# Which half of the tokens is combined first in the tail of a decoder layer, and how the gates of the dense experts are built

## The reference

```python
def peer_ffn(xf, w_query, keys1, keys2, expert_u, expert_v):
    def block(xt):                                    # 128 tokens
        qry = (xt @ w_query).reshape(PEER_BLOCK, PEER_HEADS, 2, PEER_KEY_DIM)
        s1 = jnp.einsum('thd,kd->thk', qry[:, :, 0], keys1)
        s2 = jnp.einsum('thd,kd->thk', qry[:, :, 1], keys2)
        v1, i1 = lax.top_k(s1, PEER_TOPK)
        v2, i2 = lax.top_k(s2, PEER_TOPK)
        cand_s = (v1[..., :, None] + v2[..., None, :]).reshape(PEER_BLOCK, PEER_HEADS, PEER_TOPK * PEER_TOPK)
        cand_i = (i1[..., :, None] * PEER_KEYS + i2[..., None, :]).reshape(...)
        top_s, pos = lax.top_k(cand_s, PEER_TOPK)
        idx = jnp.take_along_axis(cand_i, pos, axis=-1)
        gate = jax.nn.softmax(top_s.astype(jnp.float32), axis=-1).astype(xt.dtype)
        act = jax.nn.gelu(jnp.einsum('td,thkd->thk', xt, expert_u[idx]))
        return jnp.einsum('thk,thkd->td', gate * act, expert_v[idx])
```

## Time and profile before

| what | value |
|---|---|
| median of the timed runs | 4261.98 us |
| the profiled execution's own time | 4251.53 us |
| its span (what all rows below refer to) | 4249.7 us |
| PE busy | 3756.1 us, 88% |
| DVE busy | 2619.1 us, 62% |
| POOL busy | 1856.3 us, 44% |
| ACT busy | 811.9 us, 19% |
| moved by DMA | 1063.93 MB, 250 GB/s on the mean |
| software (indirect) DMA | 537.08 MB |

### The profile page before, as it was taken

One profiled execution on the slowest core, in us unless ns is written; L12 is line 12 of the kernel. 1 busy time (PEld: TensorE's weight loads), 2 busy tenths in 40 slices (PEclk: granted clock), 3 DMA queues, 4 the chain that ended last, 5 costly groups with the idle time before them and its releaser, 6 DMA issues. The chain is left out here.

```text
span 4249.7 us, 42972 instructions
## 1 busy us (share of the span) xinstructions
PE 3756.1 (88%) x15498; PEld 2778.5 (65%) x15498; DVE 2619.1 (62%) x5356; ACT 811.9 (19%) x1637; POOL 1856.3 (44%) x1714
## 2 busy tenths in 40 slices
PE   8889998978999999993697899989789999999935
PEld 7546787867766666641585467877676666666424
DVE  5765216645577677788657652166456776677876
ACT  2243302224000000000222532022240000000002
POOL 6102004764455455567370020047645554555663
PEclk9889999989999999996798999999899999999967
DMA  3201144558999999999722012345579999999996
GB/s 103 109 30 40 66 139 119 125 142 268 376 406 409 409 407 409 407 397 378 266 82 109 31 39 76 139 119 124 159 253 397 405 410 409 401 409 409 399 381 253
DMA packets 333955, 1063.93 MB, mean 250 GB/s; under 512 B 79152, under 2 KB 96176, under 8 KB 312496
## 3 DMA queue, kind: packets, MB, share of 16 engines
q0 software_dynamic: 184320, 537.08, 34.5%
q1 hardware_dynamic: 132368, 505.22, 31.5%
q10 hardware_dynamic: 17056, 18.88, 1.3%
HBM read 1025.27 MB, written 35.78 MB: 250 GB/s over the span
## 5 line engine op out<-in xcount | busy, mean ns | idle before, releaser
L2091 POOL DMA_INDIRECT u_rows<-in_peer_u,idx_all x512 | 662.7, 1294 | 681.1 <-DVE act_u L1990 564.3
L1657 PE MATMUL bank<-v_tile,shared 128*128 128x512 f32 x2048 | 904.6, 597 | 25.3 <-DVE shared L2032 22.5
L2002 DVE SCALAR_TENSOR_TENSOR x<-v_rows,act_w,x 128x1024 f32<-128x1024 f32 x512 | 657.9, 1285 | 345.0 <-DMA v_rows<-in_peer_v,idx_all 325.9
L2091 POOL DMA_INDIRECT v_rows<-in_peer_v,idx_all x512 | 545.7, 1066 | 402.2 <-DVE x L2002 309.8
L1657 PEld LDWEIGHTS bank<-v_tile,shared 128*128 128x128 f32 x2048 | 392.0, 192 | 476.5 <-issue 444.3
L1990 DVE CUSTOM_DVE_ANT_0 u_rows<-u_rows,h 128x1024 f32<-128x1024 f32 x512 | 609.2, 1223 | 146.1 <-DMA u_rows<-in_peer_u,idx_all 144.7
L2101 POOL DMA_INDIRECT first_cells<-first_gate,cell_all x256 | 412.1, 1610 | 578.0 <-DVEq L1982 465.3
L1645 PE MATMUL bank<-hT,bT 128*128 128x256 f32 x2048 | 454.4, 381 | 0.0
L1645 PEld LDWEIGHTS bank<-hT,bT 128*128 128x128 f32 x2048 | 391.1, 191 | 73.6 <-issue 23.9
L1549 PE MATMUL bank<-hT,ring 128*128 128x256 f32 x1536 | 341.3, 384 | 14.2 <-PEq L150 14.2
L1549 PEld LDWEIGHTS bank<-hT,ring 128*128 128x128 f32 x1536 | 294.3, 193 | 55.9 <-issue 15.8
(11 more groups left out here) (377 smaller groups left out, 4998.9 us busy)
## 6 DMA issues: line engine op xcount, KB each, us to landing
v_tile<-in_peer_v SPq DMA_DIRECT2D x256, 512.0 KB, 7.5
ring<-in_w_in_panels SPq DMA_DIRECT2D x76, 1024.0 KB, 4.9
bT<-in_peer_ut SPq DMA_DIRECT2D x128, 512.0 KB, 7.5
ring<-in_peer_w_query SPq DMA_DIRECT2D x32, 1024.0 KB, 5.0
aT<-in_peer_ut SPq DMA_DIRECT2D x64, 512.0 KB, 6.9
sT<-in_peer_ut SPq DMA_DIRECT2D x64, 512.0 KB, 6.8
ring<-in_ple_w_gate SPq DMA_DIRECT2D x24, 1024.0 KB, 8.4
first_cells<-zeros SPq DMA_DIRECT2D x16, 1024.0 KB, 11.4
```

What stands on the lines that cost most here:

```text
L1657: ins = mm(acc[t][part][:, :], act_pair[p % AHEAD][:, at:at + P], v_tile[:, e % DENSE, part * 512:part * 512 + 512], start=(e == 0), stop= ...
L2002: stt(out=m.x[:, 2 + t, :], in0=vr[:, n % RINGS, :], scalar=act_w[:, p % 4, i:i + 1], in1=m.x[:, 2 + t, :], op0=ALU.mult, op1=ALU.add).the ...
L2091: nc.gpsimd.indirect_dma_start(out=rows[:, n % RINGS, :], out_offset=None, in_=table, in_offset=bass.IndirectOffsetOnAxis(ap=idx_all[:, t, ...
```

## The change

1. Half 1, the gathered one, is combined first. Its first two heads are chosen early in the combination of half 0, so that chunks 0 to 10 stand between the steps of that combination and chunk 11 behind its norm. The fetches of POOL stand in the same places of the list.
2. The eight heads of half 0 are then chosen in a row, with six `pre` between them.
3. Both tiles of half 0 get their gates from one-hot products: 64 quads instead of 32, with two chunks between them. The scatter, the cell numbers and the zeros are gone, and the reads of the scattered table too. DVE now compares and scales in one instruction per token; every third quad's other side is made by ACT (Square, then Relu of one minus it).
4. The third head of half 1 is chosen among the six late `pre`; chunks 15 to 65 follow with the 64 pairs as before, so 41 chunks instead of 52 stand beside the pairs.
5. ACT's gelu of a chunk is moved one chunk later in the list. DVE applies the gates of a pair in one instruction instead of two, and SP loads the first two groups of gates after `pre` 8.

The core of the diff:

```diff
-QUADS = P // 4
-HOT_CHUNKS = 4
+QUADS = 2 * P // 4
+HOT_CHUNKS = 15
+ACT_QUAD = 2
 LAG = 2
+GATES_AFTER = 8
+GATHER, DENSE_HALF = 1, 0
+FIRST_HEADS = 2
...
+    g, d = steps[GATHER], steps[DENSE_HALF]
+    order = g + d[0:1] + [("norm", GATHER)] + d[1:2] + [("query", GATHER, 0), ("query", GATHER, 1)] + d[2:3] + [("score", GATHER, 0)]
+    order += choose(GATHER, 0) + d[3:5] + [("score", GATHER, 1)] + choose(GATHER, 1) + d[5:6] + chunk(0) + d[6:7] + chunk(1)
+    begun = 2
+    for n in range(7, 20):
+        order += d[n:n + 1]
+        if n % 4 != 2 and n != 11:
+            order += chunk(begun)
+            begun += 1
+    order += [("norm", DENSE_HALF), ("query", DENSE_HALF, 0), ("query", DENSE_HALF, 1), ("score", DENSE_HALF, 0)] + chunk(begun)
+    begun += 1
     pairs = 0
+    for head in range(PEER_HEADS):
+        order += [("query", DENSE_HALF, head + 2)] if head + 2 < PEER_HEADS else []
+        order += [("score", DENSE_HALF, head + 1)] if head + 1 < PEER_HEADS else []
+        order += choose(DENSE_HALF, head)
+        if pairs < EARLY:
+            order.append(("pre", pairs))
+            pairs += 1
+    order.append(("slots",))
     for q in range(QUADS):
         order.append(("hot", q))
+        if q % 20 == 19 and begun < HOT_CHUNKS - 1:
+            order += chunk(begun)
+            begun += 1
+    order += [("hot", QUADS), ("query", GATHER, FIRST_HEADS), ("score", GATHER, FIRST_HEADS)]
     for p in range(pairs, AHEAD):
         order.append(("pre", p))
+        if p == GATES_AFTER:
+            order.append(("first_gates",))
+        if p == pairs + 1:
+            order += choose(GATHER, FIRST_HEADS)
...
@@ hot, on ACT
-                    act.wait_ge(s.left_ready, q + 1)
+                k = q + 2
+                if k < QUADS and by_act(k):
+                    if k >= 4:
+                        act.wait_ge(s.hot_filled, k - 3)
+                    tile, at = k // (P // 4), 4 * k % P
                     for i in range(4):
-                        at = 4 * q + i
-                        f(left[q % 4][:, i, :], left[q % 4][:, i, :], ACT.Copy, scale=turned_sel[:, 2, at:at + 1]).then_inc(s.left_scaled, 1)
+                        f(right[k % 4][:, i, :], m.c("iota"), ACT.Square, scale=-1.0, bias=turned_sel[:, tile, 0, at + i:at + i + 1]).then_inc(s.right_squared, 1)
+                    act.wait_ge(s.right_squared, 4 * right_made(k)[1])
+                    f(right[k % 4], right[k % 4], ACT.Relu, scale=-1.0, bias=1.0).then_inc(s.right_acted, 1)
@@ hot, on DVE
-                tt(left[q % 4], over(turned_sel[:, 1, at:at + 4].unsqueeze(2), (P, 4, P)),
-                   over(m.c("iota").unsqueeze(1), (P, 4, P)), ALU.is_equal).then_inc(s.left_ready, 1)
-                tt(right[q % 4], over(turned_sel[:, 0, at:at + 4].unsqueeze(2), (P, 4, P)),
-                   over(m.c("iota").unsqueeze(1), (P, 4, P)), ALU.is_equal).then_inc(s.right_ready, 1)
+                for i in range(4):
+                    ts(left[q % 4][:, i, :], m.c("iota"), turned_sel[:, tile, 1, at + i:at + i + 1], first_gate[:, tile, at + i:at + i + 1],
+                       ALU.is_equal, ALU.mult).then_inc(s.left_ready, 1)
+                if not by_act(q):
+                    tt(right[q % 4], over(turned_sel[:, tile, 0, at:at + 4].unsqueeze(2), (P, 4, P)),
+                       over(m.c("iota").unsqueeze(1), (P, 4, P)), ALU.is_equal).then_inc(s.right_ready, 1)
@@ on POOL
-            late = TOPK * (PEER_HEADS - 1)
-            for n in range(late):
-                scatter(n)
```

More of the change, by code:

```diff
@@ L1368, in tail_order @@
[L1368 to L1385, removed]
@@ L1387, in tail_order @@
-    pairs = 0
+    place = {what: k for k, what in enumerate(CHOSEN)}
+    choose = lambda half, head: [("choose", place[half, head], part) for part in range(4)]
+    beside = {}
+    for head in range(FIRST_HEADS + 2, PEER_HEADS):
+        at = HEAD_CHUNKS * (head - 1) - (4 if head == PEER_HEADS - 1 else 0)
+        beside.setdefault(at - 5, []).append(("query", GATHER, head))
+        beside.setdefault(at - 2, []).append(("score", GATHER, head))
+        for part in range(4):
+            beside.setdefault(at + part, []).append(("choose", place[GATHER, head], part))
@@ new lines, in chunk @@
+    def chunk(c):
+        return beside.pop(c, []) + [("chunk", c)]
+    g, d = steps[GATHER], steps[DENSE_HALF]
[7 more added lines that the diff above has]
+            begun += 1
@@ L1396, in tail_order @@
     for p in range(pairs, AHEAD):
         order.append(("pre", p))
+        if p == GATES_AFTER:
+            order.append(("first_gates",))
+        if p == pairs + 1:
+            order += choose(GATHER, FIRST_HEADS)
+    while begun < HOT_CHUNKS:
+        order += chunk(begun)
+        begun += 1
+    for n, what in enumerate([("query", GATHER, FIRST_HEADS + 1), ("score", GATHER, FIRST_HEADS + 1)] + choose(GATHER, FIRST_HEADS + 1)):
+        beside.setdefault(begun + n, []).append(what)
     after = {DENSE_END: [("add",), ("embed", 0)], DENSE_END + 1: [("scale", 0), ("turn", 0)], DENSE_END + 2: [("turned", 0)]}
@@ L1558, in mix @@
             def mix(half, pair):
-                if half == 0 and pair == 0:
+                if rank(half) == 0 and pair == 0:
                     pe.wait_ge(s.wg_in, 16)
@@ L1582, in norm @@
             def norm(half):
-                for t in range(2 * half, 2 * half + 2):
-                    pe.wait_ge(s.h_ready, t + 1)
+                for t in range(2):
+                    pe.wait_ge(s.h_ready, 2 * rank(half) + t + 1)
                     for part, banks in ((0, to_act), (1, to_vec)):
@@ L1593, in query @@
             def query(half, head):
-                if half == 0 and head == 0:
+                if rank(half) == 0 and head == 0:
                     pe.wait_ge(s.keys_in, 16 * 2)
@@ L1751, in _ @@
             loads = iter(range(len(sources)))
-            parts = {"gate": panel, "mix": panel, "out": panel, "query": panel, "embedded": panel, "pre": pre, "values": values, "add": add}
+            parts = {"gate": panel, "mix": panel, "out": panel, "query": panel, "embedded": panel, "pre": pre,
+                     "first_gates": first_gates, "values": values, "add": add}
             for what, *n in order:
@@ L2117, in _ @@
                     fetch(n, s.v_free, vr, tables[1], m.v_landed)
-                if c < LATE_CHUNKS:
-                    for n in range(TOPK // LATE_CHUNKS):
-                        scatter(late + c * TOPK // LATE_CHUNKS + n)
+            parts = {"norm": norm, "chunk": chunk}
+            for what, *n in order:
+                if what in parts:
+                    parts[what](*n)
     clear(nc, s)
```

199 lines of the change are left out of this document (77 added, 122 removed).

## The result

The changed kernel takes 4428.02 us, the median of four runs (4427.25 to 4432.55), against 4261.1 for the kernel before on the same chip: 1.0395 times as long, interval 1.0377 to 1.0413. The forecast was 4290, with a range up to 4350. So the direction came true, and the change was +167 us where the sum had +28, six times as much.

The account below looks back on a forecast made before the run. DMA was taken to hold PE back by some 52 us in the pairs. Per layer +101 - 42 - 45 = +14, +28 for two on 4251.5, gave 4280, as a median 4290; own range 4262 to 4320, with rivals 4210 to 4350.

Parts of the forecast that it names:

- the sum: All terms of a layer's tail together: +101 - 42 - 45 = +14 us, for two layers +28.
- The first combination and the first choice: Start of the tail: combination unchanged, first choice about 15 us later, near 2802; the mix costs PE about 11 us.
- The second combination: Combination with early chunks: DVE's order binds, 146 us, plus 18 for DMA, up to 3010; then eight choices, quads from 3142.
- rival 4: Second combination: gathers beside it crawl, so it doesn't overlap as said; chance 0.07 together with rival 3.
- The quads: 64 quads at 1.3 us, with chunks, cold starts and staging waits 106 us, bounds 76 and 155.
- rival 3: Quads: the clock stays low throughout, 149 us instead of 106, +57 a layer, 4376; chance 0.07 together with rival 4.
- From the quads to the first `values`: Behind the quads: a query, a score and seven `pre` pairs on PE take 56 us, up to 3304.
- the front: Start of the tail to the first `values`: 101 us later per layer, at 3304 against 3202.7.
- the term of -42: Stage of pairs: PE becomes the bound at 795 us, with 10 allowed for late tiles, against 847 taken.
- The term of -45: Behind PE's last product: the dense sums are added on DVE 2 us later instead of 47.
- Rival 2: Stage of pairs: DMA stays the bound, PE loses 30 us, sums 15 later; 4380, half of it 4335; chance 0.11.
- Rival 1: Quads: they run at PE's own pace, 76 us instead of 106; 4230, or 4194 clear of the DMA limit; chance 0.32.

Follow-up runs that it names:

- c1: a3 with 6 instead of 15 early chunks ahead of the pairs: 4381.39 us, ratio 1.0296.
- c3: a3 with three of four parts of the last four dense choices left out (computes other gates, only prices the choices): 4309.89 us, ratio 1.0128.
- e1: a3 with the chunk ahead of the first dense choice and the two in the quads moved behind the quads: 4352.53 us, ratio 1.0234.
- a1_goal: The changed kernel with chunks 15 to 56 and the pairs spread by PE's work (a pair with `pre` counts 2, without 1): 4366.89 us, ratio 1.0266.
- a2: The changed kernel with the gelu back in its own chunk's place from chunk 15 on: 4421.34 us, ratio 1.0387.
- a3: The changed kernel with the edits of a1_goal and a2 together: 4362.35 us, ratio 1.0251.
- b1: The kernel before with only the gelu of a gathered chunk one chunk later on ACT: 4256.66 us, ratio 1.0004.
- e3: e1 with the last pair at chunk 58 instead of 56 and every second instead of every third right side of the quads on ACT: 4311.59 us, ratio 1.0133.
- b3: The new gates alone (64 quads, no scatter, joined gate product) in the order of the kernel before, gelu in its chunk's place: 4321.44 us, ratio 1.0149.

## Why the prediction was wrong, step by step

- *The first combination and the first choice*: right. The first choice began 196.6 us into the tail (2897.3 less 2700.7), forecast 192.3; the wait at the mix was 10.16 us where I had 11.
- *The second combination*, limited by DVE and somewhat by DMA: right in kind. The first dense choice began 409.5 us into the tail (3110.24 less 2700.7), forecast 400.3, and DVE waited 17.1 us in the combination for gathered rows, 3.3 at most in one wait, where the forecast added 18 for DMA; so rival 4 (gathers that crawl) fell too. From there to the quads 127.6 us were taken, forecast 132. The quads began 537.1 us into the tail (3237.8 less 2700.7), forecast 532.3 (3142 less 2609.7). The chunks in the combination are not free (33 us for nine, c1), and the eight choices in a row are DVE's (c3), both as argued.
- *The quads*: 113 us against 106. The new operation took 0.26 us from start to start and not 0.17; the two chunks cost their full 10.2 us each and not 8 (e1). The granted clock was 0.84 in the stage: 16 instructions at 3276 us took 3.79 us behind 7.91 us of idle, against 2.02 us at 3263 behind 1.18. It fell in single places and did not stay low, so rival 3 (149 us) fell.
- *From the quads to the first `values`*: 57 us, forecast 56. In all the front came out at +114 against +101. This was the largest term, and it was off by 13.
- **The step that failed** is the first sum, "115 x 6.91 = 795 us, against 847 taken. So DMA holds PE back by some 52 us." It counted only `pre` and `values` of PE's work. The queries and scores in the same stretch, some 40 us, raise PE's floor to 831; the term of -42 (52 less 10 allowed for late tiles, which the run did not need) became -17.
- **The second failure** is "chunks 54 to 56 (13 MB, 31 us) fit as well into the 795, so the sums are added 2 us behind PE": a load averaged over the stage. The average does fit, into the 831 us that PE takes, as a1_goal shows (0.1 us behind). But the list binds each chunk to a pair, the last 12 pairs take half the time, and there DMA stood at 1.01: from 4142 us to the sums DVE waited 34.5 us for gathered rows. The term of -45 became -13.
- *Rival 2* named the room that DVE can't use early, and was priced at 4335 to 4380 with a chance of 0.11. Its mechanism (gates loaded one group ahead, tiles late beside the gathers) is not what the runs show: PE lost nothing, only the sums came late, by 32 us and not 15. The late gelu, costed at nothing, is worth 3 to 7 us at most (a2, a3, with intervals that overlap), and nothing on the kernel before (b1).
- *Rival 1* (quads at PE's own pace) fell: DVE sets the pace at 1.44 us a quad, and e3 shows that moving more to ACT does not help.

The two failed terms are 25 and 32 us, the front 13: 70 a layer, 140 for two, of the 138 by which 4290 missed. With the two gains at the size that they had, and the forecast's own front, the sum would have been 101 - 17 - 13 = +71 a layer, +142 and not +28. Why the whole is slower than before follows from b3 and a1: 64 us from the gates (32 more quads in a row on a bound DVE), and some 105 from the order, of which 55 to 61 are only the spread of the chunks. That the rest, 45 to 50, is the row of choices less what early chunks bring is worked out from c1 and c3, not shown by a run of its own.

## What to carry to other kernels

To say how far a stage is from its engine's floor, sum every instruction of that engine in that stretch by the view that groups them, not only those of the loop one thinks of; the rest was 5% here and nearly as large as the expected gain. The idle time that the same view gives (11.7 us here) is a first measure of what can be won: the 17 us that the stage became shorter are near it, the 52 of the forecast are not. Where one list paces two streams of work, a load that fits on the average must fit in each part: look for the place where one stream's steps get shorter. And work moved under an engine that has time over is cheap only until its new neighbours are bound by the same engine: nine chunks beside the combination cost 3.7 us each, the one in DVE's wait for a score nothing, two among the quads 10.2 each.

## What the runs showed of the hardware

A DVE tensor_scalar over 128 columns of float32 with two per-partition numbers showed as 335 to 341 ns long on the mean and 0.26 us from start to start, so 128 columns cost nearly half of the 0.60 us that a 512-column comparison of two tensors takes in the rows of e1_chunks_out. The joined gate product of 512 columns took 686 ns, against 421 and 426 for its two halves before. The Trainium skill, TensorE: Matmul & The Clock Gate, in its section on HAM oscillation, says that bursts between idle gaps start at half clock; the trace agrees at the first quads behind the wait for the choices and behind the two chunks (3.75, 3.79 and 3.45 us for 16 instructions, 2.02 between). The clock also fell at three places behind shorter idle times, and e1_chunks_out, without the chunks, kept it behind an idle time as long as one of these: 16 instructions took 3.65 us behind 1.92 us in the changed kernel, and 2.02 us behind 1.92 us in e1_chunks_out. So the length of the idle time just before does not decide it alone, and what does stays open here. The granted clock of the stage was 0.84 with the two chunks and 0.97 without them:

```profile
3197.00:3290.00 93.00, 67.67 (x515) 63.27 (x516) 90.22 (x295) 70.44 (x165) 0.00 (x0) 0.97 0.47 159
```

DMA moved between 395 and 413 GB/s in every stretch read with a share of 1.01 or more, with queues of gathered rows and of whole tiles side by side.
